# One attention stage, four edits: a rotation moved behind block 6, the scale folded into weights, the maximum taken negated, one gate product a head

## The chip, the cores and the metric

The kernel runs on one core of one Trainium2 chip. The metric is the device time of one launch in microseconds, the median of several runs. The engines are TensorE (PE, with its weight loads as PEld), VectorE (DVE), ScalarE (ACT), GpSimd (POOL) and SyncE (SP), which here only issues DMAs.

## What is computed

Two layers of a hybrid decoder trunk, 512 tokens, model width 2048, float32. Each layer adds to x the output projection of three branches that all come from one input projection of RMSNorm(x): latent attention times silu of a gate, a convolution of 31 taps times silu of a gate, and a state-space branch (SSD). The part that the change touches is the attention of 6 heads:

```python
q = rms_norm(q, q_norm); k = rms_norm(k, k_norm)          # per head, 128 + 64 features
q = concat([q[..., :128], rope(q[..., 128:])]); k likewise
sc = einsum('bqhd,bkhd->bhqk', qi, k) * scale              # query blocks of 128
sc = where(mask, sc, -inf)
p = softmax(sc)
o = einsum('bhqk,bkhd->bqhd', p, v)
o_mla = o * silu(g_mla)
```

## The kernel before

Activations lie with features on the 128 partitions and the 512 tokens along the row. All weights stream from HBM in units of 128 x 1024 float32. SyncE loads a unit into one of 2 stage buffers; ScalarE writes its rounded part `whi` (line 731) and VectorE the rest, `wlo` (line 958), into a ring of 3; TensorE then does 24 products of 128x512 for it (lines 480 to 482: high times high, low times high, high times low). The split of unit u+3 stands at the head of step u on ScalarE and VectorE and waits until TensorE has used unit u.

One hand-written list, `STEPS`, sets the order on all engines. `hooks()` hangs tasks behind the halves of the input projection's tiles: `put(u, task)` puts a task behind half-tile u (a tile has two halves, u = 2j and 2j+1). In each engine's program the tasks of one half-tile come in the order in which they were put. Before the attention, three pairs of heads are projected ("proj"), their squares are summed ("head_sum"), the norms applied ("head_apply", lines 1185 to 1194), and the position features rotated ("rotate", lines 1195 to 1198: five products and a sum on VectorE; `qk_ready` then lets TensorE use that pair).

The attention is a pipeline of 24 blocks (n = 4 times head plus query block; 4 to a head, 8 to a pair), one behind each half-tile from 28 on, with two more steps to drain it. The score width is 128, 256, 384, 512 for n mod 4 = 0 to 3. In step n ("attend", n):

- TensorE, behind the 24 products of the half-tile: the scores of block n into bank S[n % 2] (lines 611, 612), the transposes of the probabilities of block n-1 (line 620, waits for `prob_ready`), and the product with the values of block n-2 into its 128 columns of the one bank O (line 633). For every block it waits until the block before has been taken from O (`o_taken`, line 631).
- VectorE: adds the mask to the diagonal block (line 1205), takes the row maximum (line 1206), multiplies it by minus the scale (line 1207, `max_ready`), multiplies O's 128 columns of block n-2 with the gate (line 1212, `o_taken`), and takes the reciprocal of the row sum (line 1217). From block 6 on it also does 2 taps of the 31-tap convolution at up to three places of a step (line 1006). From block 15 on, each odd step also evacuates and finishes a tile of the state-space input (lines 1144 and 1043).
- ScalarE: exp with the scale and the bias (line 863), the copy of the transposed block n-1 out of PSUM (line 871), and the probabilities times the reciprocal (line 875).

Blocks 0 to 15 need the rotations of pairs 0 and 1; block 16 is the first that needs the rotation of pair 2 (the pair kept in `xg` and `key2`). That rotation is put behind half-tile 29, where it comes ahead of step 1 of the attention. Its queue on VectorE is: split of unit 32, evacuation and silu of the tile, rotation, step 1.

After the attention, GpSimd waits for the last `o_taken` and then loads `acsb` for the first SSD chunk (line 452), on which VectorE and ScalarE wait.

`half_taps` (line 1010) halves the parameters of the short convolution once a layer, ahead of that layer's work.

Of the kernel before, what the change touches and what calls it, by code (L numbers as in the profile page):

```python
# [21 lines left out]
ALU = mybir.AluOpType  # L22
ACT = mybir.ActivationFunctionType
AX_X = mybir.AxisListType.X

P = 128
# [41 lines left out]
def hooks():  # L68

    h = {}  # L70

    def put(u, *task):
        h.setdefault(u, []).append(task)

    put(4, "rx")
    put(8, "cq_sum")
    put(12, "ckv_sum")
    put(13, "v", 0)
    put(14, "v", 1)
    put(15, "kd_turn")  # L80
    put(17, "acs")
    put(19, "acs_turn")
    for p in range(3):
        put(18 + 4 * p, "head_sum", p)
        put(19 + 4 * p, "head_apply", p, 0)
        put(20 + 4 * p, "head_apply", p, 1)
        put(21 + 4 * p, "rotate", p)
    for p in range(3):
        put(16 + 4 * p, "proj", p)
    for u in range(28, 54):  # L90
        put(u, "attend", u - 28)
    for s in range(8):
        put(54 + 2 * s, "ssd_a", s)
        put(56 + 2 * s, "ssd_b", s)

    for u in range(56, 70, 2):
        h[u].sort(reverse=True)
    put(71, "ln_mean")
    put(73, "ln_var")
    for f in range(4):  # L100
        put(77 + f, "pw", f)
    return h
# [96 lines left out]
def hybrid_kernel(nc, x, weights, params, consts, out, acs_rows):  # L199
    ctx = ExitStack()  # L200
    with ctx:
# [104 lines left out]
        def par(name, i=0, n=1):  # L306
            at = PARAM_COLS[name][0] + i
            return pv[:, at:at + n]

        def sig(name, per_layer, credit=0):  # L310
            return Signal(nc, ctx, name, per_layer, credit)
# [57 lines left out]
        probT_done = sig("probT_done", 24)  # L369
        probT_taken = sig("probT_taken", 24)  # L370
        o_done = sig("o_done", 24)
        o_taken = sig("o_taken", 24)
        tap3_done = sig("tap3_done", 10)
        xb_ready = sig("xb_ready", 10)
        ssd_turned = sig("ssd_turned", 8)
# [49 lines left out]
        @block.gpsimd  # L425
        def _(pool):
            pool.sem_inc(x_free.sem, 1)

            def go():

                pool.sem_inc(pool_go, 1)


            for layer in range(DEPTH):
                for name, args, own in STEPS:
                    if name == "acs_turn":
                        pool.wait_ge(acs48_ready.sem, acs48_ready.at(layer, 1))
                        go()
                        pool.dma_start(acs_rows, acs48).then_inc(acs_stored.sem, 16)
                        pool.wait_ge(acs_stored.sem, acs_stored.at(layer, 16))  # L440
                    if name == "ssd_a":
                        s = args[0]
                        g, c = s // NT, s % NT
                        if s == 0:

                            pool.wait_ge(o_taken.sem, o_taken.at(layer, 24))
                        else:

                            pool.wait_ge(ssd_in.sem, ssd_in.at(layer, s))
                        rows = acs_rows[12 * c + 6 * g:12 * c + 6 * g + 6, :].rearrange("(o h) l -> o (h l)", o=1)  # L450
                        go()
                        pool.dma_start(acsb[:, :, :].rearrange("p h l -> p (h l)"),
                                                      rows.to_broadcast([P, GH * P])).then_inc(acsb_loaded.sem, 16)
                    if name == "out2" and args[0] < 2 or name == "out" and args[1] == 0:
                        f = args[0]
                        if f == 0:

                            pool.wait_ge(ssd_taken.sem, ssd_taken.at(layer, 8))
                        if f >= 2:

                            pool.wait_ge(acc_taken.sem, acc_taken.at(layer, len(TILES) + f - 1))
                        go()
                        pool.dma_start(xr[f % 2][:, :], (out if layer else x)[:, f * SEQ:(f + 1) * SEQ]).then_inc(res_loaded[f % 2].sem, 16)
                        if f >= 2:
                            pool.wait_ge(x_ready.sem, x_ready.at(layer, f - 1))
                            go()
                            pool.dma_start(out[:, (f - 2) * SEQ:(f - 1) * SEQ], xg[:, f - 2, :]).then_inc(x_stored.sem, 16)
                for f in (KX - 2, KX - 1):
                    pool.wait_ge(x_ready.sem, x_ready.at(layer, f + 1))
                    go()  # L470
                    pool.dma_start(out[:, f * SEQ:(f + 1) * SEQ], xg[:, f, :]).then_inc(x_stored.sem, 16)

                pool.wait_ge(x_stored.sem, x_stored.at(layer, 16 * KX))
                pool.sem_inc(x_free.sem, 1)

        @block.tensor
        def _(pe):
# [13 lines left out]
            for layer in range(DEPTH):  # L491
# [7 lines left out]
                for name, args, own in STEPS:  # L499
# [100 lines left out]
                    elif name == "attend":  # L600
# [21 lines left out]
                        if 2 <= n:  # L622
                            m = n - 2
                            qb, hh = m % 4, m // 4
                            pe.wait_ge(probT_taken.sem, probT_taken.at(layer, m + 1))
                            if m == 0:

                                pe.wait_ge(acs48_ready.sem, acs48_ready.at(layer, 1))
                            else:

                                pe.wait_ge(o_taken.sem, o_taken.at(layer, m))
                            for kb in range(qb + 1):
                                last = full(O[:, qb * P:(qb + 1) * P], value[:, kb, hh * P:(hh + 1) * P],
                                            probT[m % 2][:, kb * P:(kb + 1) * P], kb == 0, kb == qb)
                            last.then_inc(o_done.sem, 1)
# [36 lines left out]
                    elif name == "pw":  # L672
                        f, u = args[0], own[0]
                        bank = [O, M][f % 2]
                        if f == 0:
                            pe.wait_ge(o_taken.sem, o_taken.at(layer, 24))
                            pe.wait_ge(conv_r.sem, conv_r.at(layer, 1))
                        if f >= 2:
                            pe.wait_ge(pw_taken.sem, pw_taken.at(layer, f - 1))
# [31 lines left out]
        def _(act):  # L711
# [3 lines left out]
            for layer in range(DEPTH):  # L715
                def a(signal, out, in_, func, **more):

                    signal = signal or act_chain
                    nc.scalar.activation(out, in_, func, **more).then_inc(signal.sem, 1)  # L719
                    act.wait_ge(signal.sem, signal.next())  # L720
# [54 lines left out]
                for name, args, own in STEPS:  # L775
# [79 lines left out]
                    elif name == "attend":  # L855
                        n = args[0]
                        if n < 24:
                            width = (n % 4 + 1) * P
                            act.wait_ge(max_ready.sem, max_ready.at(layer, n + 1))
                            if n >= 2:  # L860

                                act.wait_ge(probT_done.sem, probT_done.at(layer, n - 1))
                            a(exp_done, prob[n % 2][:, 0:width], S[n % 2][:, 0:width], ACT.Exp, scale=SCALE,
                              bias=negm, accum_out=rsum)
                        if 1 <= n <= 24:
                            m = n - 1
# [50 lines left out]
        def _(dve):  # L917
# [7 lines left out]
            for layer in range(DEPTH):  # L925
                def d(signal, ins, go=False):

                    signal = signal or dve_chain
                    ins.then_inc(signal.sem, 1)
                    value = signal.next()  # L930
                    if not go:
                        dve.wait_ge(signal.sem, value)
# [9 lines left out]
                def ts(signal, out, x, s1, op0, s2=None, op1=None, go=False):  # L942
                    if op1 is None:
                        d(signal, nc.vector.tensor_scalar(out, x, s1, None, op0), go)  # L944
                    else:
                        d(signal, nc.vector.tensor_scalar(out, x, s1, s2, op0, op1), go)
# [63 lines left out]
                def half_taps(layer):  # L1010

                    dve.wait_ge(params_ready.sem, params_ready.at(layer, 1))
                    ts(None, par("scw", 0, 10 * SSD_K + 10), par("scw", 0, 10 * SSD_K + 10), 0.5, ALU.mult)

                def x_lo(k, layer):

# [58 lines left out]
                for name, args, own in STEPS:  # L1075
# [123 lines left out]
                    elif name == "attend":  # L1199
                        n = args[0]  # L1200
                        if n < 24:
                            qb, width = n % 4, (n % 4 + 1) * P
                            dve.wait_ge(scores_done.sem, scores_done.at(layer, n + 1))
                            diag = S[n % 2][:, qb * P:(qb + 1) * P]
                            tt(None, diag, diag, mask, ALU.add)
                            d(None, nc.vector.tensor_reduce(rmax, S[n % 2][:, 0:width], AX_X, ALU.max))
                            ts(max_ready, negm, rmax, -SCALE, ALU.mult)
                        if 2 <= n:
                            m = n - 2
                            h, q = m // 4, slice((m % 4) * P, (m % 4 + 1) * P)  # L1210
                            dve.wait_ge(o_done.sem, o_done.at(layer, m + 1))
                            tt(o_taken, xg[:, h, q], O[:, q], xg[:, h, q], ALU.mult)
                        if n < 24:
                            if n >= 6:
                                convolve(2)
# [216 lines left out]
```

## Time and profile before

| what | us |
|---|---|
| median of 3 runs (1669.96 to 1671.18) | 1670.09 |
| the profiled execution | 1675.85 |
| its span | 1674.1 |
| TensorE busy, 94% of the span | 1570.2 |
| VectorE busy, 64% | 1072.6 |
| ScalarE busy, 36% | 610.3 |

The profile is one execution. Times of rows count from the start of its span; the first layer's attention runs from about 231 to 433 us, the second's from about 1057 to 1258 us. Matmuls are pipelined and their ends are modelled, so that the distance between starts says more than a duration. The granted clock is given as a share of 2.4 GHz: 1.00 and 0.50 (1.2 GHz) are its two levels.

### The profile page before, as it was taken

How to read it: one execution, taken by the hardware profiler on the slowest of the kernel's cores; microseconds unless marked ns; L12 is line 12 of the kernel's file. 1: busy time of each engine (PE TensorE's matmuls, PEld its weight loads, DVE VectorE, ACT ScalarE, POOL GpSimd, SP SyncE). 2: the span in 40 equal slices, each digit the busy share in tenths (PEclk: the TensorE clock that was granted, in tenths of full speed). 3: DMA queues.
4: the chain of work that ended last, by engine and by line, in shares of the span. 5: the costliest groups of instructions: out<-in, count | busy, mean ns of one | idle time of the engine just before them, and what ended most of it. 6: DMA issues, size and time to landing. Idle time of an engine off the chain costs nothing.

```text
span 1674.1 us, 18545 instructions
## 1 busy us (share of the span) xinstructions
PE 1570.2 (94%) x7062; PEld 1248.1 (75%) x7062; DVE 1072.6 (64%) x1746; ACT 610.3 (36%) x847; POOL 44.6 (3%) x86
## 2 busy tenths in 40 slices
PE   6999989999989779999999999899999798799997
PEld 5877767777867667888877877677777686678886
DVE  7445674899999656533454467558999985573221
ACT  6444443344333234222244354433443332352220
POOL 0000000000000000101000000000000000001010
PEclk9999999999999889999999999899999898899999
DMA  5322222222322213445422222122113232125441
GB/s 209 100 85 89 76 88 63 65 74 64 95 75 99 85 51 104 134 144 151 142 85 85 80 97 88 63 70 69 64 63 104 83 104 70 57 83 167 141 151 63
DMA packets 44423, 158.13 MB, mean 94 GB/s; under 512 B 5520, under 2 KB 5808, under 8 KB 44336
## 3 DMA queue, kind: packets, MB, share of 16 engines
q1 hardware_dynamic: 36720, 129.64, 24.0%
q0 software_dynamic: 6464, 23.12, 4.9%
q10 hardware_dynamic: 1152, 4.19, 0.6%
q8 instruction: 56, 0.92, 0.2%
q14 instruction: 31, 0.25, 0.0%
HBM read 148.50 MB, written 8.44 MB: 94 GB/s over the span
## 4 chain that ended last, share of the span: by engine, by line
PE 69%; DVE 19%; ACT 8%; issue 3%; DMA 1%; DVEq 0%; SPq 0%; ACTq 0%; POOL 0%; POOLq 0%
PE acc L480 14%; PE acc L481 14%; PE acc L482 14%; PE S L480 3%; PE S L482 3%; PE S L481 3%; PE S L485 3%; DVE wlo L958 3%; ACT whi L731 3%; DVE xb L949 3%; DVE cacc L1006 3%; PE T L480 2%; PE T L482 2%; PE T L481 2%; ACT L719 1%
## 5 line engine op out<-in xcount | busy, mean ns | idle before, releaser
L480 PE MATMUL acc<-hhi,whi 128*128 128x512 f32 (+1 forms) x1504 | 610.4, 406 | 35.3 <-DVE wlo L958 35.3
L958 DVE TENSOR_TENSOR wlo<-stage,whi 128x1024 fp32r<-128x1024 f32 (+3 forms) x252 | 300.3, 1196 | 469.4 <-ACT whi L731 467.6
L481 PE MATMUL acc<-hlo,whi 128*128 128x512 f32 (+1 forms) x1504 | 595.0, 396 | 0.0
L482 PE MATMUL acc<-hhi,wlo 128*128 128x512 f32 (+1 forms) x1504 | 594.4, 395 | 0.0
L731 ACT ACTIVATE whi<-stage 128x1024 fp32r<-128x1024 f32 (+3 forms) x252 | 259.6, 1036 | 519.1 <-PE acc L482 302.4
L480 PEld LDWEIGHTS acc<-hhi,whi 128*128 128x128 f32 (+1 forms) x1504 | 287.2, 191 | 100.3 <-DVE wlo L958 36.9
L482 PEld LDWEIGHTS acc<-hhi,wlo 128*128 128x128 f32 (+1 forms) x1504 | 286.6, 191 | 64.2
L481 PEld LDWEIGHTS acc<-hlo,whi 128*128 128x128 f32 (+1 forms) x1504 | 287.3, 191 | 63.2 <-issue 3.9
L1006 DVE SCALAR_TENSOR_TENSOR cacc<-glu,pv,cacc 128x512 f32<-128x512 f32 x240 | 171.7, 748 | 4.6
L480 PE MATMUL S<-hhi,whi 128*128 128x512 f32 x192 | 75.5, 393 | 0.0
L482 PE MATMUL S<-hhi,wlo 128*128 128x512 f32 x192 | 74.7, 389 | 0.0
L481 PE MATMUL S<-hlo,whi 128*128 128x512 f32 x192 | 74.7, 389 | 0.0
L719 ACT ACTIVATE prob<-S,cols 128x128 f32<-128x128 f32 (+3 forms) x48 | 25.4, 528 | 131.9 <-DVE cols L944 131.9
L719 ACT ACTIVATE temp<-temp 128x512 f32<-128x512 f32 x48 | 30.3, 631 | 109.9 <-DVEq L936 109.9
L480 PE MATMUL T<-hhi,whi 128*128 128x512 f32 x128 | 49.8, 389 | 0.0
L481 PE MATMUL T<-hlo,whi 128*128 128x512 f32 x128 | 49.8, 389 | 0.0
L482 PE MATMUL T<-hhi,wlo 128*128 128x512 f32 x128 | 49.8, 389 | 0.0
L719 ACT ACT_TABLE_LOAD x37 | 47.5, 1283 | 5.5 <-issue 4.9
L949 DVE SCALAR_TENSOR_TENSOR xb<-raw,pv,xb 128x512 f32<-128x512 f32 x60 | 45.1, 752 | 2.7
L485 PE MATMUL S<-qk 64*128 64x128 f32 (+7 forms) x128 | 45.9, 457 | 0.0
L481 PEld LDWEIGHTS S<-hlo,whi 128*128 128x128 f32 x192 | 36.0, 188 | 7.9 <-issue 0.5
L480 PEld LDWEIGHTS S<-hhi,whi 128*128 128x128 f32 x192 | 36.0, 188 | 7.9 <-issue 0.5
(226 smaller groups left out, 1599.5 us busy)
## 6 DMA issues: line engine op xcount, KB each, us to landing
stage<-weights SPq DMA_DIRECT2D x236, 512.0 KB, 3.4
y_features<-xg POOLq DMA_DIRECT2D x32, 256.0 KB, 4.1
acsb<-acs_rows POOLq DMA_DIRECT2D x16, 384.0 KB, 4.3
xg<-x_features ACTq DMA_DIRECT2D x8, 512.0 KB, 11.3
xr<-x_features POOLq DMA_DIRECT2D x16, 256.0 KB, 4.2
xr<-y_features POOLq DMA_DIRECT2D x16, 256.0 KB, 4.0
stage<-weights SPq DMA_DIRECT2D x8, 256.0 KB, 2.7
stage<-weights SPq DMA_DIRECT2D x4, 384.0 KB, 3.0
```

The source lines that it names most:

```text
L480: nc.tensor.matmul(out, a, c, start=start, stop=False)
L481: nc.tensor.matmul(out, a, d, start=False, stop=False)
L482: return nc.tensor.matmul(out, b, c, start=False, stop=stop)
L485: return nc.tensor.matmul(out, a, b, start=start, stop=stop)
L719: nc.scalar.activation(out, in_, func, **more).then_inc(signal.sem, 1)
L731: nc.scalar.activation(whi[u % RING][:, 0:w], stage[u % STAGE][:, 0:w], ACT.Copy).then_inc(hi_done.sem, 1)
L949: d(signal, nc.vector.scalar_tensor_tensor(out=out, in0=x, scalar=s, in1=y, op0=op0, op1=op1), go)
L958: nc.vector.tensor_tensor(wlo[u % RING][:, 0:w], stage[u % STAGE][:, 0:w], whi[u % RING][:, 0:w].bitcast(F32), ALU.subtract).then_inc(lo_d ...
L1006: ins = nc.vector.scalar_tensor_tensor(out=cacc[:, j, :], in0=src, scalar=wt, in1=cacc[:, j, :], op0=ALU.mult, op1=ALU.add)
```

## The change

Four edits. The rotation of pair 2 goes from behind half-tile 29 (ahead of step 1) to behind half-tile 33, where it follows step 5. The softmax scale is multiplied into the query norm's weights in `half_taps`, and no longer given to exp. The row maximum is written negated by the reduction itself, so that the product of line 1207 falls away. The gate product is done once a head, over the 512 columns of O, in steps 5, 9, ... 25, where there were four of 128 columns in steps 2 to 25; TensorE waits for it only at a head's first block.

```diff
-        put(21 + 4 * p, "rotate", p)
+        if p < 2:
+            put(21 + 4 * p, "rotate", p)
...
     for u in range(28, 54):
         put(u, "attend", u - 28)
+    put(33, "rotate", 2)
...
-        o_taken = sig("o_taken", 24)
+        o_taken = sig("o_taken", HEADS)
...
-                            pool.wait_ge(o_taken.sem, o_taken.at(layer, 24))
+                            pool.wait_ge(o_taken.sem, o_taken.at(layer, HEADS))
...
-                                pe.wait_ge(o_taken.sem, o_taken.at(layer, m))
+                                pe.wait_ge(o_taken.sem, o_taken.at(layer, m // 4))
...
-            a(exp_done, prob[n % 2][:, 0:width], S[n % 2][:, 0:width], ACT.Exp, scale=SCALE,
+            a(exp_done, prob[n % 2][:, 0:width], S[n % 2][:, 0:width], ACT.Exp,
                               bias=negm, accum_out=rsum)
...
                     ts(None, par("scw", 0, 10 * SSD_K + 10), par("scw", 0, 10 * SSD_K + 10), 0.5, ALU.mult)
+                    ts(None, par("qn", 0, 2), par("qn", 0, 2), SCALE, ALU.mult)
...
-                            d(None, nc.vector.tensor_reduce(rmax, S[n % 2][:, 0:width], AX_X, ALU.max))
-                            ts(max_ready, negm, rmax, -SCALE, ALU.mult)
-                        if 2 <= n:
-                            m = n - 2
-                            h, q = m // 4, slice((m % 4) * P, (m % 4 + 1) * P)
-                            dve.wait_ge(o_done.sem, o_done.at(layer, m + 1))
-                            tt(o_taken, xg[:, h, q], O[:, q], xg[:, h, q], ALU.mult)
+                            d(max_ready, nc.vector.tensor_reduce(negm, S[n % 2][:, 0:width], AX_X, ALU.max, negate=True))
+                        if n >= 5 and n % 4 == 1:
+                            h = n // 4 - 1
+                            dve.wait_ge(o_done.sem, o_done.at(layer, n - 1))
+                            tt(o_taken, xg[:, h, :], O[:, :], xg[:, h, :], ALU.mult)
```

## Rows read from the trace of the kernel before

**Rows 1.** Waits of TensorE over the whole span: total us, times, longest.
```profile
PE T L620 <- ACT prob L719: 12.0, 8, 3.9
```

**Rows 2.** Busy time by stretch: PE, PEld, DVE, ACT, POOL, clock, DMA share, GB/s.
```profile
345.00:432.00 87.00, 85.83 (x394) 64.89 (x393) 79.98 (x145) 36.81 (x64) 0.00 (x0) 1.00 0.21 66
...
1170.00:1257.00 87.00, 86.11 (x394) 65.05 (x393) 80.22 (x145) 36.71 (x64) 0.00 (x0) 1.00 0.20 65
```

**Rows 3.** Timeline of VectorE, first layer, steps 0 and 1: start, duration, instruction.
```profile
238.58 0.30 DVE L940 TENSOR_TENSOR S<-S,const 128x128 f32<-128x128 f32 x1
...
245.15 3.55 DVE L940 TENSOR_TENSOR temp<-xg,const 128x512 f32<-128x512 f32 x5
...
249.46 0.30 DVE L940 TENSOR_TENSOR S<-S,const 128x128 f32<-128x128 f32 x1
```

**Rows 4.** Timeline of TensorE, first layer: steps 1 to 3, then steps 6 and 7.
```profile
240.70 0.33 PE L620 MATMUL T<-const,prob 128*128 128x128 f32 x1 [1.94 <-ACT prob L719]
246.36 1.65 PE L485 MATMUL S<-qk 128*128 128x384 f32 x4
251.92 0.69 PE L620 MATMUL T<-const,prob 128*128 128x128 f32 x2 [3.92 <-ACT prob L719]
260.40 2.07 PE L485 MATMUL S<-qk 128*128 128x512 f32 x4
...
285.32 0.44 PE L620 MATMUL T<-const,prob 128*128 128x128 f32 x2
291.30 1.02 PE L485 MATMUL S<-qk 128*128 128x512 f32 x2
```

**Rows 5.** Timeline of TensorE, second layer, steps 1 to 3.
```profile
1066.05 0.35 PE L620 MATMUL T<-const,prob 128*128 128x128 f32 x1 [1.92 <-ACT prob L719]
1073.28 1.65 PE L485 MATMUL S<-qk 128*128 128x384 f32 x4
...
1077.27 0.69 PE L620 MATMUL T<-const,prob 128*128 128x128 f32 x2 [2.34 <-ACT prob L719]
...
1086.05 2.07 PE L485 MATMUL S<-qk 128*128 128x512 f32 x4
```

**Rows 6.** Stretch behind the long wait of the first layer, columns as in rows 2.
```profile
253.00:254.00 1.00, 1.00 (x4) 0.81 (x3) 0.94 (x1) 0.00 (x0) 0.00 (x0) 0.50 0.00 0
```

**Rows 7.** Timeline of VectorE, first layer, steps 5 to 8.
```profile
282.50 0.16 DVE L1217 RECIPROCAL cols<-cols 128x1 f32<-128x1 f32 x1 [0.42 <-ACT prob L719]
285.18 1.23 DVE L958 TENSOR_TENSOR wlo<-stage,whi 128x1024 fp32r<-128x1024 f32 x1 [2.52 <-ACT whi L731]
...
290.00 0.15 DVE L1217 RECIPROCAL cols<-cols 128x1 f32<-128x1 f32 x1
...
292.67 1.23 DVE L958 TENSOR_TENSOR wlo<-stage,whi 128x1024 fp32r<-128x1024 f32 x1 [1.06 <-ACT whi L731]
...
301.00 1.23 DVE L958 TENSOR_TENSOR wlo<-stage,whi 128x1024 fp32r<-128x1024 f32 x1 [1.79 <-ACT whi L731]
```

**Rows 8.** Timeline of TensorE, first layer, step 7.
```profile
293.31 0.55 PE L620 MATMUL T<-const,prob 128*128 128x128 f32 x3
```

**Rows 9.** Groups of VectorE instructions by shape: busy us, mean ns, idle before.
```profile
L940 DVE TENSOR_TENSOR xg<-O,xg 128x128 f32<-128x128 f32 x48 | 14.0, 291 | 1.8 <-DVE cols L944 0.3
...
L944 DVE TENSOR_SCALAR cols<-cols 128x1 f32<-128x1 f32 x48 | 7.4, 154 | 1.6
...
L940 DVE TENSOR_TENSOR xg<-S,xr 128x512 f32<-128x512 f32 x8 | 5.5, 684 | 3.1 <-PE S L482 3.1
```

**Rows 10.** Timeline of ScalarE, end of the first layer's attention.
```profile
431.71 1.06 ACT L731 ACTIVATE whi<-stage 128x1024 fp32r<-128x1024 f32 x1 [3.05 <-PE acc L482]
```

**Rows 11.** The chain that ended last, entry to the first SSD chunk.
```profile
439.41 0.30 DVE xg L940
...
440.31 3.51 DMA acsb<-acs_rows
```

**Rows 12.** Timeline of VectorE, start of the span.
```profile
7.47 0.75 DVE L1018 SCALAR_TENSOR_TENSOR hlo<-xg,pv,hhi 128x512 fp32r<-128x512 f32 x1 [0.64 <-ACT hhi L745]
```

More of the change, by code:

```diff
@@ L675, in _ @@
                         if f == 0:
-                            pe.wait_ge(o_taken.sem, o_taken.at(layer, 24))
+                            pe.wait_ge(o_taken.sem, o_taken.at(layer, HEADS))
                             pe.wait_ge(conv_r.sem, conv_r.at(layer, 1))
```

## The prediction

> **What bounds the kernel now.** I read the list of TensorE's waits first, since TensorE is busy for 94% of the span and nearly every microsecond it stands still is one of the kernel. One line there belongs to the attention: the transposes of the probabilities waited 12.0 us in 8 places for ScalarE's last step of the softmax [rows 1]. Then I looked each of these places up in TensorE's timeline. Two are at the start of each layer's attention: 1.94 and 3.92 us in the first layer [rows 4], 1.92 and 2.34 us in the second [rows 5]. That is 10.12 of the 12.0 us. The others are small and lie late in the attention, where VectorE is busy 80 of 87 us and TensorE stands still for 87.00 - 85.83 = 1.17 us in the first layer and 0.89 us in the second [rows 2]. Next I asked VectorE's timeline what makes the two early waits. The first: the mask of block 0 starts only at 238.58, because the norms of pair 2 are ahead of it, and TensorE goes on at 240.70 [rows 3, 4]. The second: from 245.15 on VectorE does the rotation of pair 2, and only at 249.46 the mask of block 1; TensorE goes on at 251.92 [rows 3, 4]. Last I read the clock by stretches: behind the long wait it is 0.50, that is 1.2 GHz [rows 6], so a wait costs more than its length.
>
> **The rotation, taken from ahead of step 1.** It holds VectorE from 245.15 to 249.46, 4.31 us. From the mask of block 1 to the transposes it is 251.92 - 249.46 = 2.46 us, two engines passing the block to and fro. With the rotation gone the mask starts at 245.15, and the probabilities are ready at 245.15 + 2.46 - 0.19 = 247.42 (the 0.19 is the product that falls away, below). TensorE reaches this place at 251.92 - 3.92 = 248.00. So the wait goes as a whole, with 0.6 us to spare.
>
> What the wait drags behind it is read from distances. From these transposes to the scores of block 3 is 260.40 - 251.92 = 8.48 us; the same work in steps 6 and 7 takes 291.30 - 285.32 = 5.98 us [rows 4]. The difference, 2.50 us, is the slow clock. First layer: 3.92 + 2.50 = 6.42 us. In the second layer the distance is 1086.05 - 1077.27 = 8.78, so 2.80 us; its wait is only 2.34, because TensorE comes late to it: already behind the first wait its step takes 1073.28 - 1066.05 = 7.23 us, where the first layer needs 246.36 - 240.70 = 5.66 [rows 4, 5]. That slow stretch of 1.57 us belongs to the first wait, which the change leaves. Second layer: 2.34 + 2.80 = 5.14 us. Together 11.56 us.
>
> **The rotation, put behind step 5.** VectorE is through with step 5 at 282.66 and then waits 2.52 us for the next weights [rows 7]. The rotation would end at 282.66 + 4.31 = 286.97, and the split that stood at 285.18 is 1.79 us late. Queued behind it: the taps, the mask and maximum of block 6, its reciprocal. That reciprocal stands at 290.00; 1.8 us late, and allowing 1 us for ScalarE's last step behind it, the probabilities are there at 292.8, and TensorE wants them at 293.31 [rows 7, 8]. Step 6 itself becomes shorter by 0.5 us (below), and VectorE's idle times ahead of the next two splits, 1.06 and 1.79 us, take up what is left [rows 7]. The weights are not missed either: the late split is of unit 37, in step 34, three units ahead of its use. So I cost the new place at nothing. Its bound: without this cover, 1.8 us a layer and no more, as the rest fits into the 2.52 us of idle time. The rotation is needed first by block 16, ten steps later. It issues no DMA, and no queue but VectorE's holds it.
>
> **The negated maximum.** 48 products of 154 ns fall away [rows 9], each 0.19 us with the gap to the next start. In most steps nothing waits for them. In step 0 they are on the path: the first wait of each layer becomes 0.19 us shorter, 0.38 us together. A negating reduction is not in this trace. It may cost nothing, or at the worst as much as the product that it replaces, 0.15 us; I take nothing, since it is one instruction over the same elements. Exp without a scale is the same instruction.
>
> **One gate product a head.** Four of 291 ns become one of about 684 ns, by the product of the same shape that reads another PSUM bank [rows 9]. With gaps of 0.04 us, a head's 1.32 us become 0.72 us. In a step with the product VectorE has 0.4 us more and the negation's 0.2 us less; in the three others 0.5 us less. Over eight steps that is 8 x 0.19 + 8 x 0.33 - 2 x 0.72 = 2.7 us. Late in the attention VectorE and TensorE run neck and neck: TensorE there lost 1.17 and 0.89 us to VectorE's lateness [rows 2], less than VectorE saves. I take all of it, 2.06 us. Bounds: nothing, if the lateness comes from elsewhere, and 2.06. TensorE's new wait, at a head's first block, comes a whole unit after VectorE's product and costs nothing.
>
> The last product costs. It lies on the chain, ahead of the load for the first SSD chunk [rows 11]: 0.68 instead of 0.29 us, twice, 0.79 us. Before it, ScalarE waited 3.05 us for TensorE's last unit of the attention [rows 10], so what TensorE wins up to here is handed to VectorE, and the SSD part and the rest of the layer follow as they did.
>
> **The folded scale** is one small product a layer. In the first layer VectorE then waits 0.64 us for ScalarE anyhow [rows 12]; in the second it falls into the output projection, paced by TensorE. Nothing.
>
> **Sum:** 11.56 + 0.38 + 2.06 - 0.79 = 13.2 us. The profiled execution, 1675.85 us (span 1674.1), would be 1662.6. It was 5.8 us longer than the median of the runs; I take the same difference from the median: 1670.1 - 13.2 = 1656.9 us.
>
> **A rule of the skill weighed.** The first wait, of nearly the same length, left the clock at full speed in one layer and cost 1.57 us in the other [rows 4, 5]. The Trainium skill (TensorE: Matmul & The Clock Gate, "The HAM clock gate") says that the gate's observation runs free of the kernel, so that the same kernel has more slow matmuls in one run than in another. This agrees with the two layers. By it neither layer's first wait is sure to cost or not to cost, and the gain would lie anywhere between 11.6 and 14.8 us. My sum keeps the fates that the trace shows.
>
> **Rivals.**
> 1. *The early wait goes, but the clock falls otherwise.* If both first waits cost 1.57 us, the gain is 11.6 us (1658.5); if neither does, 14.8 (1655.3). For it: the two layers differ. It is inside my forecast's own range.
> 2. *VectorE is the bound behind block 5.* The 1.8 us come through in each layer, and the late waits stay: 13.2 - 3.6 - 2.1 = 7.5 us, 1662.6. For it: the cover at block 6 is only about 0.5 us. Against it: idle time in the next steps. 10%.
> 3. *The early wait is replaced.* The probabilities of block 1 come just 0.6 us ahead of need. If something else holds VectorE or ScalarE there, such as the split of unit 33, a wait of 1 to 2 us remains with a slow clock of 2.5 us: about 4 us a layer are kept back, 1665. Against it: that split is queued behind the block on both engines. 4%.
> 4. *The stall only moves, and it is slower.* One mechanism: the rotation behind step 5 holds block 6 until TensorE waits for it at 293.31 with the clock falling. The price is up to 4.31 us of wait and 2.8 of clock a layer, against 6.42 and 5.14 won: with the last gate product 2 x 7.1 + 0.8 - 11.6 - 0.4 = 3.0 us slower, 1673. It decides only if the idle 2.52 us ahead of the split can't be used, and block 6 comes over 4 us late; the rows give 1.8. 3%.
> 5. *Nothing measurable:* the executions without a profile don't have the early stalls at this size, since they are 5.8 us shorter. 5%.
> 6. *More than the sum:* the lateness of VectorE in the late steps is larger than TensorE's idle time shows, as ends are modelled; 16 to 18 us, 1653. 6%.
>
> **How the numbers follow.** The forecast has 72%: 1656.9, its own range 1655 to 1659.5. The range for 8 in 10 adds the bounds of the late waits and part of rivals 2 and 6: 1653 to 1661.5. About 0.2% (3.3 us) can be told from no change. Faster: 72 + 10 + 4 + 6 = 92%; within: 5%; slower: 3%.
>
> **What would show it.** In the changed kernel's profile: no mask of block 1 behind six rotation instructions, and the transposes of block 1 without a wait in both layers; the first waits at 1.75 us; full clock from 248 us on in the first layer; the split behind step 5 some 1.8 us late against TensorE and no wait at block 6; TensorE without gaps from block 15 to 23; the last gate product at 0.68 us just ahead of the load for the SSD part. The forecast is wrong if a wait of over a microsecond stands at blocks 1, 6 or 7, or if the clock still drops to 0.50 behind step 2.

## The result, and the profile after

The changed kernel took 1663.19 us (median of 5 runs, 1662.32 to 1664.54) where the kernel before took 1671.18 us (5 runs, 1669.96 to 1674.75): 8.0 us less, ratio 0.9949, 95% interval 0.9934 to 0.9964. Forecast were 1656.9 us and a range of 1653 to 1661.5. The direction was right, the time lies above the range.

Trace against trace it looks otherwise. The execution traced of the kernel before took 1675.85 us, the one of the changed kernel 1663.19 us: 12.7 us, against a sum of 13.2. So the first question was where the 4.7 us between the two comparisons lie.

The waits of the transposes in TensorE's list of waits, changed kernel: total us, times, longest.

```profile
PE T L622 <- ACT prob L721: 3.5, 2, 1.8
```

The line that had 12.0 us in 8 places [rows 1] has two left, the first wait of each layer. TensorE's timeline at the start of the first layer's attention, to be held against [rows 4]:

```profile
240.98 0.36 PE L622 MATMUL T<-const,prob 128*128 128x128 f32 x1 [1.75 <-ACT prob L721]
...
248.23 1.65 PE L487 MATMUL S<-qk 128*128 128x384 f32 x4
249.81 0.44 PE L622 MATMUL T<-const,prob 128*128 128x128 f32 x2
```

The transposes of block 1 no longer wait: 8.83 us behind those of block 0, where it was 11.22. But from block 0 to the scores of block 2 it is 248.23 - 240.98 = 7.25 us, which was 5.66 in the first layer of before [rows 4]: the first wait has now cost the clock here as well. The stretch behind it (PE, PEld, DVE, ACT, POOL busy, clock, DMA share, GB/s):

```profile
242.00:244.00 2.00, 2.00 (x6) 1.60 (x5) 1.83 (x2) 0.01 (x1) 0.00 (x0) 0.50 0.03 8
```

VectorE's timeline around the rotation's new place, and TensorE's transposes of blocks 5 and 6, to be held against [rows 7, 8]:

```profile
278.29 3.55 DVE L942 TENSOR_TENSOR temp<-xg,const 128x512 f32<-128x512 f32 x5
281.88 0.69 DVE L942 TENSOR_TENSOR xg<-temp,temp 128x512 f32<-128x512 f32 x1
282.60 1.23 DVE L960 TENSOR_TENSOR wlo<-stage,whi 128x1024 fp32r<-128x1024 f32 x1
...
288.84 1.23 DVE L960 TENSOR_TENSOR wlo<-stage,whi 128x1024 fp32r<-128x1024 f32 x1 [0.32 <-ACT whi L733]
...
296.41 1.23 DVE L960 TENSOR_TENSOR wlo<-stage,whi 128x1024 fp32r<-128x1024 f32 x1 [1.55 <-ACT whi L733]
```
```profile
280.73 0.44 PE L622 MATMUL T<-const,prob 128*128 128x128 f32 x2
288.72 0.55 PE L622 MATMUL T<-const,prob 128*128 128x128 f32 x3
```

The split stood 0.14 us ahead of the transposes of block 5 and now stands 1.87 us behind them, so it is 2.0 us late; the next idle time shrinks from 1.06 to 0.32 us, the one after is 1.55 us, and block 6 has no wait. Late in the attention TensorE has no idle time left (before: 1.17 and 0.89 us [rows 2]). The row is of the first layer; from 1165 to 1245 us, in the second, TensorE is busy for 80.00 us too:

```profile
345.00:425.00 80.00, 80.00 (x369) 61.17 (x368) 72.78 (x120) 34.91 (x61) 0.00 (x0) 1.00 0.22 71
```

VectorE's groups by shape, against [rows 9]: the group of 16 products of 512 columns, 12 of them the new gate products, has a mean of 689 ns (684 forecast), and the negating reduction of 256 columns 424 ns, the mean of the plain one before as well.

```profile
L942 DVE TENSOR_TENSOR xg<-O,xg 128x512 f32<-128x512 f32 x16 | 11.0, 689 | 0.4
...
L1209 DVE TENSOR_REDUCE cols<-S 128x1 f32<-128x256 f32 x12 | 5.1, 424 | 0.4
```

The entry to the first SSD chunk in the chain, against [rows 11]:

```profile
433.24 0.70 DVE xg L942
...
433.98 0.57 issue
434.55 3.51 DMA acsb<-acs_rows
```

From ScalarE's split at the end of the attention (425.54 us, 431.71 before [rows 10]) to VectorE's first use of `acsb` (438.08, 443.85 before) it is 12.54 us instead of 12.14. In the second layer the same distance is 1257.04 - 1244.50 = 12.54 us instead of 1269.35 - 1257.10 = 12.25. So the last gate product costs 0.40 and 0.29 us.

### The profile page after: what moved, and what is told of

Its sections match the earlier page's. It is cut to its first block, busy times and chain, and to the rows that moved or that the text cites. A ratio compares the mean times of both kernels' runs of the same rounds, so it can differ in the third digit from the quotient of the medians.

```text
span 1661.4 us, 18427 instructions
## 1 busy us (share of the span) xinstructions
PE 1566.3 (94%) x7062; PEld 1246.0 (75%) x7062; DVE 1060.2 (64%) x1664; ACT 610.3 (37%) x847; POOL 44.6 (3%) x86
## 4 chain that ended last, share of the span: by engine, by line
PE 78%; DVE 12%; ACT 6%; issue 2%; DMA 1%; DVEq 0%; SPq 0%; ACTq 0%; POOL 0%; POOLq 0%
PE acc L482 17%; PE acc L483 17%; PE acc L484 17%; PE S L487 5%; PE S L482 3%; PE S L483 3%; PE S L484 3%; PE T L483 2%; PE T L484 2%; PE T L482 2%; DVE wlo L960 2%; DVE xb L951 2%; PE O L487 2%; ACT whi L733 1%; PE T L622 1%
## 6 DMA issues: line engine op xcount, KB each, us to landing
xg<-x_features ACTq DMA_DIRECT2D x8, 512.0 KB, 11.3
```

## The experiments

The attention of each traced kernel can be cut at the starts of the transposes. All such distances below are worked out from TensorE's timeline, one traced execution a row; T0 to T23 are the transposes of blocks 0 to 23, in us, first layer / second layer. The column T0 is the start in the first layer.

| kernel | T0 | T0 to T1 | T1 to T2 | T2 to T7 | T14 to T23 |
|---|---|---|---|---|---|
| before | 240.70 | 11.22 / 11.22 | 10.48 / 10.78 | 37.96 / 37.96 | 69.66 / 69.39 |
| before, again | 243.83 | 11.22 / 11.23 | 10.43 / 7.96 | 37.95 / 37.99 | 69.65 / 69.38 |
| changed | 240.98 | 8.83 / 8.83 | 7.99 / 7.98 | 37.97 / 37.98 | 68.15 / 68.16 |
| changed, again | 243.80 | 7.24 / 8.79 | 7.99 / 7.99 | 37.97 / 37.97 | 68.15 / 68.15 |
| rotation moved only | 243.82 | 7.22 / 8.81 | 7.98 / 7.99 | 37.98 / 37.97 | 69.66 / 69.39 |
| rotation stays | 240.54 | 11.04 / 11.03 | 10.64 / 9.49 | 37.96 / 37.96 | 68.15 / 68.15 |
| gate once a head only | 241.46 | 11.22 / 11.22 | 7.97 / 9.25 | 37.97 / 37.96 | 68.26 / 68.25 |
| maximum negated only | 241.12 | 11.03 / 11.03 | 9.33 / 9.38 | 37.96 / 37.96 | 68.15 / 68.15 |
| before, waits filled | 242.29 | 11.23 / 11.23 | 7.99 / 7.98 | 37.98 / 37.99 | 69.65 / 69.41 |
| changed, wait filled | 240.93 | 7.22 / 7.21 | 7.98 / 7.99 | 37.97 / 37.97 | 68.16 / 68.16 |
| key norm behind step 0 | 240.00 | 7.22 / 7.21 | 7.99 / 7.98 | 37.97 / 37.97 | 68.15 / 68.16 |
| rotation behind block 14 | 241.76 | 8.83 / 8.84 | 7.99 / 7.99 | 37.97 / 37.97 | 69.96 / 69.97 |
| rotation's products twice | 241.25 | 8.82 / 7.22 | 7.98 / 7.98 | 42.21 / 40.26 | 68.15 / 68.16 |

T7 to T14 is 54.78 or 54.79 us in all of them.

**1. The two kernels again.** No edit. 

> The kernel before, unchanged, as its own control. The question: the trace of before was an execution of 1675.85 us, 4.7 us longer than the median of its runs, while that of the changed kernel was an execution at its median; trace against trace the change gave 12.7 us, median against median 8.0. Theory A (the executions of before scatter over some 5 us, the changed one less so, since what the early waits cost depends on where the clock falls): runs between 1669.5 and 1676, and a second trace whose early stretch differs from the first by microseconds of slow clock. Theory B (the earlier runs of before were made on another chip or at another hour, and here all lie near 1674.5): runs within 1.5 us of each other at 1674 to 1675, against 1663 for the change, so that its gain is 11 to 12 us.

> The changed kernel, unchanged, beside the kernel before on the same chip. Theory A: gain 8 us (ratio 0.995). Theory B: gain 11 to 13 us (ratio 0.9925 to 0.993). In both: no wait at block 1, first wait 1.75 us, as in its trace.

Measured on one chip: the kernel before over 23 runs 1669.34 to 1679.22 us, median 1674.2; its copy over 12 runs 1669.76 to 1679.15, median 1675.09, ratio 0.9998 (0.9983 to 1.0012). The changed kernel 1664.36 us (1662.77 to 1665.55), ratio 0.9935 (0.9916 to 0.9954), 9.8 us less than the 23 runs and 10.7 less than the copy. Theory B falls, as the runs of before don't lie together. Of theory A the scatter holds: the kernel before scatters over 10 us, the changed one, with fewer runs, over 3. Its gain of 8 us was too small for this chip. In the second trace of before the second layer lost nothing behind its second wait of 2.34 us. TensorE's timeline there:

```profile
1080.45 0.44 PE L620 MATMUL T<-const,prob 128*128 128x128 f32 x2 [2.34 <-ACT prob L719]
```

The wait is as long as in the first trace [rows 5], but T1 to T2 is 7.96 us where it was 10.78. The stretch behind it ran at full clock; 1078 to 1080 us, behind the same wait of the first trace, ran at 0.50:

```profile
1081.00:1083.00 2.00, 2.00 (x10) 1.64 (x10) 1.42 (x2) 0.48 (x1) 0.00 (x0) 1.00 0.00 0
```

Also the two traces of before differ by 3.1 us ahead of T0. From 26 to 36 us, first and second trace of before:

```profile
26.00:36.00 10.00, 9.61 (x42) 7.99 (x43) 8.86 (x14) 7.59 (x13) 0.00 (x0) 1.00 0.33 107
```
```profile
26.00:36.00 10.00, 8.16 (x30) 6.51 (x29) 8.46 (x12) 7.91 (x13) 0.00 (x0) 0.83 0.31 107
```

Both stretches hold a wait of 1.83 us for the same weights, first and second trace of before:

```profile
26.39 0.47 PE L480 MATMUL acc<-hhi,whi 128*128 128x512 f32 x1 [1.83 <-DVE wlo L958]
```
```profile
27.93 0.52 PE L480 MATMUL acc<-hhi,whi 128*128 128x512 f32 x1 [1.83 <-DVE wlo L958]
```

From the end of that wait to T0 it is 214.31 and 215.90 us, so 1.59 of the 3.13 us belong to the slow clock behind it, present in one execution and not in the other. The other 1.54 us lie ahead of it: TensorE's first product starts 0.27 us later (12.31 against 12.04), and from there to this wait's end it is 15.62 us against 14.35. There 12 distances in a row from one product's start to the next are 0.43 us long in the second trace, 5 in the first, before they fall to 0.23 us; the clock column shows 1.00 in both. None of this has to do with the change, and it moves both kernels.

**2. Only the move; all but the move.** The first has the edit of `hooks()` alone, the second all others.

> Only the move of the rotation. By the prediction's sum 11.6 us of the 13.2, so nearly all of what the whole change gives on this chip; transposes of block 1 without a wait, first wait still 1.92 to 1.94 us, late waits of about 1 us a layer still there, perhaps larger by the 1.8 us that the rotation delays. Rival (VectorE is the bound behind block 5, and only the lighter steps pay for the rotation's new place): 8 us or less, with late waits of 2 us and more a layer.

> The change without the move: scale folded, maximum negated, one gate product a head, the rotation ahead of step 1 as before. By the sum 0.4 + 2.1 - 0.8 = 1.6 us faster than before; wait at block 1 still there at 3.7 to 3.9 us or its second-layer size; late waits gone. Rival (lateness at the end of the attention is VectorE's in full, ends being modelled): 3 us.

The move alone: 1666.60 us, ratio 0.9949 (0.9932 to 0.9966), 7.6 us below the median of before. That is 4 us less than the 11.6 expected and the size that the rival gave, but not by the rival's way: the late waits that its trace reports are 0.62 and 0.47 us in the first layer, as in before, where the rival wanted 2 us and more. The rest alone: 1671.47 us (1669.55 to 1675.74), ratio 0.9988 (0.9973 to 1.0002), not told from no change by its times; but its late stretch is 1.51 and 1.24 us shorter, the whole of what the full change has there, and the move takes nothing from it (69.66 and 69.39, as before). So the two parts add up: 7.6 + 2.7 = 10.3 us beside 9.8 of the whole. The rest gave 2.7 us where 1.6 were expected, near the rival's 3. No rotation comes back as lateness of VectorE.

**3. The waits filled.** Ahead of the waits of steps 1 and 2 TensorE got idle products, 7 and 15 in the kernel before, 6 and 0 in the changed one. These runs and all later ones were made on another chip than experiments 1 and 2; the kernel before had 1669.20 to 1677.06 us there over 17 runs.

```diff
+                        if n in (1, 2):
+                            for _ in range((7, 15)[n - 1]):
+                                full(M[:, :], hhi[:, 0, 0:P], hhi[:, 0, :])
```

> The kernel before, with 7 idle products ahead of the first wait of each layer and 15 ahead of the second (128x512 into bank M, which nobody reads in the attention), so that TensorE is busy through nearly all of both waits. Which VectorE chain sets the transposes of block 1 is left as it was. The theory: an execution of before loses 2.5 to 2.8 us of slow clock behind the second wait of a layer in some executions and nothing in others, which is why its runs scatter from 1669.3 to 1679.2 us. Then here the transposes of blocks 0 and 1 stay 11.2 us apart and those of blocks 1 and 2 are 8.0 us apart in both layers, and the runs lie from 1669 to 1674, a median 2 to 4 us below before. Rival (the scatter comes from elsewhere, and the slow stretch is tied to the length of VectorE's chain): 10.5 to 10.8 us apart as in the first trace, median as before.

> The changed kernel with 6 idle products ahead of the first wait (1.75 us) of each layer. If that wait's cost beyond its length is the clock's, blocks 0 and 1 are 7.2 to 7.3 us apart in both layers (they were 8.8 apart in the trace of the changed kernel, and 7.2 in the first layer of its second trace), and the median is 1 to 3 us below the changed kernel's. If the fillers only take the place of the wait and the clock was not lost in most executions: no difference.

The kernel before with filled waits, TensorE's timeline:

```profile
249.53 3.69 PE L485 MATMUL M<-hhi 128*128 128x512 f32 x15
...
253.52 0.44 PE L623 MATMUL T<-const,prob 128*128 128x128 f32 x2 [0.30 <-ACT prob L722]
259.50 2.07 PE L485 MATMUL S<-qk 128*128 128x512 f32 x4
```

VectorE's chain is untouched (T0 to T1 is 11.23 us), and from T1 to the scores of block 3 it is 259.50 - 253.52 = 5.98 us, which was 8.48 [rows 4]. Its 12 runs lie between 1669.89 and 1672.50 us, those of before beside them between 1669.20 and 1677.06, 9 of 17 above 1675. The upper group of before is gone. The runs don't fall on its lowest group (1669.2 to 1670.4 us) either, but spread from there to 1672.5; the one traced has its T0 1.6 us later than the first trace of before, with 2.12 us from the mask of block 0 to T0 in both, so the fillers don't delay it. The medians are 1671.52 and 1675.21 us, but as before jumps between its groups the ratio is 0.9991 (0.9979 to 1.0002): the ratio leaves this open, the traces and the vanished group carry it. The changed kernel with its wait filled: 1660.33 us, T0 to T1 7.2 us in both layers, 2.9 to 4.0 us below the changed kernel's two medians, at and above the upper end of what was expected. Those medians are from other sessions, so a microsecond of this may be theirs; the distances alone give 2 x 1.6 us against a trace that lost the clock in both layers.

Single runs left out, 31 of 57 runs of the kernel before and 2 of 11 with the rotation left in place lie above 1673.9 us. The kernels in which the second wait is gone or filled (changed, move only, both filled ones, key norm) have 38 runs together, and within none of their sessions do the runs lie more than 2.8 us apart. So the upper group goes with the second wait. That it is slow clock in every such run is not shown: the two traced ones had a mean granted clock of 0.970 and 0.972, but 5 of the 9 beside this experiment had 0.975, no less than the runs near 1670 us with 0.974. None of those was traced, so what they lost is open.

**4. Where the light edits count.** Each alone: the gate product only (with its waits), and the negated maximum with the folded scale only. One run each.

> Only the gate product once a head. The late stretch of each layer, from the transposes of block 14 to those of block 23, took 69.66 and 69.39 us in both traces of before and 68.15 us with the whole change and without the move. If both light edits share that gain of 1.51 and 1.23 us by the time that they take off VectorE (8 x 0.33 - 2 x 0.72 = 1.2 us against 8 x 0.19 = 1.5 us over eight steps): about 0.7 us a layer here, 68.9. If 68.15 is TensorE's own pace (its waits gone), either edit alone may reach it, and the two gains don't add.

> Only the maximum taken negated and the scale folded. First wait of each layer 0.19 us shorter (1.75 us), the maximum 0.42 us for 256 columns as without the negation. Late stretch: 68.8 us if the gain follows VectorE's saved time, 68.15 us if this edit alone is enough. Transposes of blocks 0 and 1 in both kernels 11.0 to 11.2 us apart, as the rotation is where it was.

T14 to T23 is 68.26 us with the one and 68.15 with the other, so either is nearly enough and they don't add; no kernel goes below 68.15 us, which is most likely TensorE's own pace. 1670.49 and 1670.28 us are single runs and decide nothing.

**5. How much cover the new place has.** In one kernel the rotation stands behind block 14, in the other its products are done twice.

```diff
-    put(33, "rotate", 2)
+    put(42, "rotate", 2)
```
```diff
                         q = QK[args[0]]
+                        if args[0] == 2:
+                            rope(q[2], P)
                         rope(q[2], P)
```

> The changed kernel with the rotation behind block 14 instead of block 5, where VectorE has 0.2 to 0.6 us of idle time a step instead of 2.5. If the new place costs nothing only because of the idle time that covers it, here 2 to 4 us a layer come back as waits of the transposes of blocks 15 to 23 (5 us over the two layers, 1668 beside 1663.5). Rival (VectorE has slack enough anywhere in the attention, as the lighter steps win 2.7 us a layer): under 1 us a layer.

> The changed kernel with the five products of the third rotation done twice, so that 7.9 us of VectorE stand behind step 5 instead of 4.3. It measures how much cover the place has. The single rotation made the split of unit 37 about 2 us late against TensorE and cost nothing. By the prediction the cover at block 6 ends some 0.5 us further on, so here 2 to 3 us of wait at block 6 or 7 in each layer, perhaps with slow clock behind it: blocks 2 to 7 take 40 to 43 us instead of 37.97, or 7 to 14 more than 54.79. Rival (more cover than I reckoned): both stay as they are.

The rotation behind block 14 took 1665.55 us and the doubled products 1668.01 us, single runs that decide nothing; the traces are what counts. Behind block 14 the late stretch grows by 1.81 us in each layer, and the waits are back on TensorE's timeline, 0.94 us and, one block later, 0.73 us:

```profile
359.40 0.66 PE L622 MATMUL T<-const,prob 128*128 128x128 f32 x4 [0.94 <-ACT prob L721]
```

Together that is 3.6 us, just under the 2 to 4 us a layer that were expected, and more than the rival's 1 us a layer: the place matters, but less than the 4.3 us of the rotation. With the products doubled, 3.6 us more behind step 5, block 6 waits in the first layer:

```profile
291.60 0.55 PE L622 MATMUL T<-const,prob 128*128 128x128 f32 x3 [2.56 <-ACT prob L721]
```

T2 to T7 grows by 2.29 us in the second layer, a bare wait (2.21 us), and by 4.24 in the first, where 2.56 us of wait are followed by some 1.7 us of slow clock (granted from 293 to 295 us: 0.50). Both are as expected, 2 to 3 us of wait and 40 to 43 us of distance. So 3.6 - 2.3 = 1.3 us of cover were left behind block 5.

**6. The first wait, taken away.** Block 0 doesn't need the last two products of pair 2's norms; they go behind step 0:

```diff
+    put(28, "key_apply", 2, 1)
     put(33, "rotate", 2)
...
+                        if (p, h) != (2, 1):
+                            stt(None, q[3 + h], q[3 + h], par("kn"), sqh[:, 2 + h, :], ALU.mult, ALU.mult, go=True)
+                            tt(None, q[5][r], kr2[r, :], sqh[r, 2 + h, :], ALU.mult)
+                    elif name == "key_apply":
+                        q, r = QK[2], slice(64, 128)
+                        stt(None, q[4], q[4], par("kn"), sqh[:, 3, :], ALU.mult, ALU.mult, go=True)
+                        tt(None, q[5][r], kr2[r, :], sqh[r, 3, :], ALU.mult)
```

> The changed kernel, with the last two products of the norms of pair 2 (0.75 and 0.69 us, which block 0 does not need) put behind step 0 of the attention. The mask of block 0 then starts 1.44 us earlier, and the first wait of each layer falls from 1.75 to about 0.3 us, too short to lose the clock. Expected against the changed kernel: 2 x 1.44 = 2.9 us, and 0 to 3.2 us of slow clock on top, so a median of 1658 to 1661 where the changed kernel has 1663 to 1664.5. Rival (the products only delay the split of unit 32 and block 1 behind them): blocks 0 and 1 come 1.4 us further apart, no gain.

1657.48 us (1656.10 to 1658.49), ratio to before 0.9906 (0.9887 to 0.9924). Against 1663.19 and 1664.36 us of the changed kernel it is 5.7 to 6.9 us less, the best kernel of the case; they are from other sessions, but the kernel before kept its lowest time from one chip to the next within 0.2 us. The median is 0.5 us below the range expected. The first wait is 0.26 us, and T0 to T1 is 7.2 us in both layers, so the rival, block 1 coming later instead, falls.

```profile
240.00 0.33 PE L623 MATMUL T<-const,prob 128*128 128x128 f32 x1 [0.26 <-ACT prob L722]
```

## Why the prediction was wrong, point by point

**The step that failed** is the last line of the sum: "It was 5.8 us longer than the median of the runs; I take the same difference from the median." The 13.2 us held 2.50 + 2.80 = 5.30 us of slow clock behind the second waits. These belonged to the traced execution. No run of before near 1670 us was traced, so that these don't have them is inferred, from three things: 1675.85 - 5.30 = 1670.55; the second trace less its 2.45 us of slow clock and the 3.13 us of its head gives 1675.50 - 5.58 = 1669.9; and with the waits filled the runs above 1672.5 us are gone. So I took 5.3 us from a median which didn't contain them. For that median the sum was 13.2 - 5.3 = 7.9 us, measured 8.0. That these two agree to 0.1 us is luck: the median of before was 1670.09 us in the text and 1671.18 beside the changed kernel, and two terms were off, one each way (below). The difference of 5.8 us between trace and median stood in the text, in rival 5 even as a reason, and was not asked for its cause.

**The bounds.** The text let the first wait's clock vary and took the second's as certain, since both layers of the one trace had lost it. Over the five traces with the rotation in its old place and its wait not filled (before twice, rotation stays, gate only, maximum only) T1 to T2 was, over 7.98 us, 2.50, 2.80, 2.45, 0, 2.66, 1.51, 0, 1.27, 1.35 and 1.40 us: 1.6 us in the mean. The first wait cost 1.6 us in 7 of 10 layers of the five traces that have it in full with the rotation gone. "My sum keeps the fates that the trace shows" failed here too: in the changed kernel's first trace both layers lost the clock. Trace against trace T0 to T2 became 4.88 us shorter in the first layer, forecast 6.42, and 5.19 in the second, forecast 5.14. The second layer's slow clock behind the first wait was hidden before: T0 to T1 was 11.22 us with it and without it, as VectorE's chain ended last. With the rotation gone it shows. By these means the move gives 2 x (11.22 - 7.22 - 0.7 x 1.6 + 1.6) = 9.0 us, the whole change 9.0 + 0.4 + 2.7 - 0.8 = 11.3 us; measured 8.0 and 9.8. The means of so few traces come out above both; the rest stays unexplained.

**The rotation's removal** from step 1: right. No wait at block 1.

**Its new place**: right. Forecast 1.79 us late and covered, measured 2.0 us and covered; the cover left was 1.3 us and not 0.5. Rivals 2, 3 and 4 didn't occur. Rival 2 named 1662.6 us, near the 1663.19 measured, but by a stall at block 6 and late waits that the trace doesn't have. Rival 5 took the 5.8 us for a reason to expect no gain at all; the waits were there, only their tail was not.

**The negated maximum**: right, 0.19 us off the first wait, and no price for the negation.

**The gate product**: right in mechanism. The late stretch gave 2.75 us instead of 2.06: the distance between starts shows a larger loss (1.51 and 1.24 us) than the idle time that the trace reports (1.17 and 0.89), which is rival 6, but 0.7 us of it and not 3 to 5. The last product cost 0.40 and 0.29 us, forecast 0.39. That the two light edits don't add was not foreseen and made no difference.

**The gate of the clock**: "first waits at 1.75 us" was right; "full clock from 248 us on in the first layer" too, but that trace had 0.50 from 242 to 244 us.

What stays open: what the runs of before near 1675 us with a clock of 0.975 lost, and which execution loses the clock behind a wait. The same wait of 1.75 us cost 1.6 us in one layer and nothing in the other of one execution, and nothing was tried that decides it beforehand, only fillers and shorter waits that take it away. Between T23 and the next layer's T0 the kernels scatter from 639.7 to 642.6 us; that stretch was not taken apart.

## What to carry to other kernels

A trace is one execution. Where it isn't at the median, find out what it has that the median hasn't, before a saving read from it is taken from the median. A wait's slow tail on TensorE is such a thing: count it as a range from nothing to what one trace shows, for waits removed and for waits that stay, and remember that it can be hidden while another engine's chain ends later. Work moved on an in-order engine is free where that engine waits for something else next, and doubling it is a quick way to measure how far that holds; a wait shortened to some tenths of a microsecond gave more here than its length, in the layers that had lost the clock behind it.

## What the runs showed of the hardware

The kernel before has 10 us of scatter (1669.2 to 1679.2), in groups about 2.5 to 3 us apart. At least three places make it: the head of the kernel, with 3.1 us of difference ahead of T0, about half of it slow clock behind a wait of 1.83 us and half a slow start of TensorE, and the second wait of each layer with 0 to 2.8 us. Needless matrix products in the two waits of each layer, 7 and 15 of them, brought the highest of its runs from 1677.1 to 1672.5 us, and no distance of the table became longer by more than 0.03 us. That the same wait loses the clock in one execution and not in the next (T1 to T2 of the second layer: 10.78 and 7.96 us) agrees with what the Trainium skill (TensorE: Matmul & The Clock Gate, "The HAM clock gate") says of a gate whose observation runs free of the kernel. Apart from the places with waits, the distances of the table repeat to 0.04 us from one execution to the next.
